# Rows for the experts gathered as quarter rows and turned in 32x32 blocks by VectorE

## The reference, cut to what matters

```python
def grouped_expert_mlp(h, expert, weight, w_gu, w_down):
    ...
    def expert_block(args):
        idx, e = args
        gate, up = jnp.split(h_pad[idx] @ w_gu[e], 2, axis=-1)
        return (jax.nn.silu(gate) * up) @ w_down[e]

    y = lax.map(expert_block, (slot_tok.reshape(n_blocks, MOE_BLOCK), block_e))
    y = y.reshape(-1, d) * slot_w[:, None]
    return jnp.zeros((n + 1, d), y.dtype).at[slot_tok].add(y)[:n]
```

## Time and profile before

| what | value |
|---|---|
| median of three runs | 2658.21 us |
| lowest, highest | 2656.98, 2659.9 us |
| profiled execution, span from first to last instruction | 2660.6 us |
| TensorE busy | 2561.7 us (96%) |
| VectorE busy | 1203.4 us (45%) |
| ScalarE busy | 562.7 us (21%) |
| GpSimd busy | 324.8 us (12%) |
| DMA | 590.71 MB, mean 222 GB/s |

### The profile page before, as it was taken

How to read it: one execution, slowest core, us unless ns; L and a number is a source line. 1 busy time by engine, 2 the same in 40 slices (tenths; PEclk the granted TensorE clock), 3 DMA queues, 4 the chain that set the end, 5 groups by cost and what they waited for, 6 DMA issues and landing times.

```text
span 2660.6 us, 34138 instructions
## 1 busy us (share of the span) xinstructions
PE 2561.7 (96%) x13314; PEld 1294.0 (49%) x13314; DVE 1203.4 (45%) x2576; ACT 562.7 (21%) x1181; POOL 324.8 (12%) x395
## 2 busy tenths in 40 slices
PE   6999999999999899999999899999999999999997
PEld 3444456547655444433333344577745444444333
DVE  3264357238777632222222475677787611111114
ACT  3211111028632100000000221488721000000002
POOL 0043200212011100000000012000011000000002
PEclk9999999999999999999999999899999999999998
DMA  9710111123123799999998810300024799999997
GB/s 381 306 17 0 67 48 61 35 37 88 59 104 126 292 398 420 414 378 373 411 394 334 347 51 0 71 2 2 1 76 160 271 390 423 417 423 417 407 417 263
DMA packets 99885, 590.71 MB, mean 222 GB/s; under 512 B 21727, under 2 KB 25015, under 8 KB 74761
## 3 DMA queue, kind: packets, MB, share of 16 engines
q1 hardware_dynamic: 81832, 535.72, 51.4%
q0 software_dynamic: 15296, 43.31, 4.1%
q10 hardware_dynamic: 2592, 9.44, 0.9%
HBM read 554.98 MB, written 45.99 MB: 226 GB/s over the span
## 4 chain that ended last, share of the span: by engine, by line
PE 84%; DMA 7%; DVE 6%; SPq 1%; issue 1%; POOL 0%; ACT 0%; POOLq 0%; DVEq 0%; ACTq 0%
PE PS L2702 34%; PE PS L1054 11%; PE PS L1250 5%; PE PS L1906 5%; PE PS L2139 4%; PE PS L1918 4%; PE PS L1929 4%; PE PS L1440 4%; PE PS L1723 4%; DMA ar<-in_expert_w_gu_dram 3%; DMA ar<-in_ada_w_dram 1%; PE PS L2707 1%; DMA ar<-yd 1%; DMA h2d<-ar 1%; PE PS L2712 1%
## 5 line engine op out<-in xcount | busy, mean ns | idle before, releaser
L2702 PE MATMUL PS<-ar 128*32 128x512 f32 (+2 forms) x4608 | 1012.5, 595 | 20.3 <-DMA ar<-in_expert_w_gu_dram 14.8
L2702 PEld LDWEIGHTS PS<-ar 128*32 128x32 f32 (+2 forms) x4608 | 372.2, 137 | 624.2 <-issue 616.9
L1054 PE MATMUL PS<-ar 128*128 128x512 f32 (+1 forms) x768 | 314.0, 565 | 4.2 <-DMA ar<-in_swa_w_in_dram 2.3
L2847 ACT ACTIVATE ar<-PS 128x512 f32<-128x512 f32 x48 | 28.7, 597 | 1068.3 <-PE PS L2702 1068.3
L1054 PEld LDWEIGHTS PS<-ar 128*128 128x128 f32 x768 | 144.2, 191 | 150.3 <-issue 141.5
L1962 DVE CUSTOM_DVE_ANT_0 ar<-PS,ar 128x640 f32<-128x640 f32 (+2 forms) x208 | 158.0, 797 | 71.5 <-PE PS L1906 71.3
L2139 PE MATMUL PS<-ar 128*128 128x512 f32 x392 | 175.2, 597 | 1.5 <-ACT ar L2270 0.9
L2919 DVE TENSOR_TENSOR ar<-PS,ar 128x512 f32<-128x512 f32 x48 | 33.2, 692 | 315.2 <-ACT ar L2847 315.2
L2942 DVE TENSOR_TENSOR ar<-PS,ar 128x1024 f32<-128x1024 f32 x48 | 58.8, 1225 | 242.2 <-PE PS L2702 137.1
L2925 DVE COPY ar<-PS 128x512 f32<-128x512 f32 x48 | 33.2, 692 | 279.7 <-PE PS L2712 279.7
L2017 ACT ACTIVATE ar<-ar 128x641 f32<-128x641 f32 (+4 forms) x208 | 159.5, 772 | 0.8 <-DVE ar L1962 0.8
(11 more groups left out here) (342 smaller groups left out, 2506.1 us busy)
## 6 DMA issues: line engine op xcount, KB each, us to landing
ar<-in_expert_w_gu_dram SPq DMA_DIRECT2D x128, 2048.0 KB, 16.1
ar<-in_expert_w_down_dram SPq DMA_DIRECT2D x64, 2048.0 KB, 15.5
ar<-in_ada_w_dram SPq DMA_DIRECT2D x24, 2048.0 KB, 14.7
ar<-yd SPq DMA_DIRECT2D x36, 512.0 KB, 5.4
ar<-in_ab_w_in_dram SPq DMA_DIRECT2D x6, 2048.0 KB, 9.3
h2d<-ar ACTq DMA_DIRECT2D x18, 512.0 KB, 2.9
ar<-in_x_dram SPq DMA_DIRECT2D x8, 512.0 KB, 13.5
ar<-in_ab_w_out_dram SPq DMA_DIRECT2D x1, 4096.0 KB, 27.0
```

What stands on the lines that cost most here:

```text
L1054: mm = nc.tensor.matmul(out_, lhs, rhs, start=(k == 0), stop=(k == KC - 1))
L2702: mm = nc.tensor.matmul(out[at:to], lhsT[:, at:to], w[:, k, cols], start=start, stop=stop)
```

## The change

From block 2 on a block's rows come in quarters. `h2d` is seen as 5120 rows of 1 KB. Four indirect DMAs fill `hb`: number j brings, to partition 32a + m, quarter a of the row of slot 32j + m. One VectorE transpose of 32x32 blocks then makes `hbT` of it, in place of eight transposes of TensorE and a copy from PSUM. The quarter row numbers are 4 x row + a; they are made once per layer: VectorE spreads `src_i` by a table, TensorE adds it up over the partitions (`route_fold`, four small products), and VectorE writes `src4_i` (`route_quarters`). The gated values are turned in SBUF by sixteen VectorE transposes of 32 partitions by 128 columns, in place of four of TensorE and a copy; only the last block of each layer keeps the old way. Blocks 0 and 1 keep the old way for their rows. `h2q`, `srcq` and `src4_i` are new; three small tables are added to the constants, and the semaphore counts follow.

```diff
             def turn(b):
-                pe.wait_ge(*done(f"{n}_hb{b % 2}", 16 * (b // 2 + 1)))
+                pe.wait_ge(*done(f"{n}_hb{b % 2}", hb_in(b)))
...
                 gate(b)
                 if b == 0:
                     route_shift(pe, l)
-                if b >= 1:
-                    turn_gu(b - 1)
-                if b + 1 < nb:
-                    turn(b + 1)
+                if b == 0:
+                    turn(1)
                 up(b)
+                if b == 0:
+                    route_fold(pe, l)
                 if b >= 1:
                     down(b - 1)
             if l == 1:
-                gate(nb - 1, lambda: turn_gu(nb - 2))
+                gate(nb - 1)
...
             def rows_in(b):
+                if b >= 2:
+                    dve.wait_ge(*done(f"{n}_hb{b % 2}", hb_in(b)))
+                    dve.wait_ge(*done(f"{n}_gu", b - 1))
+                    V.transpose(hbT[b % 2].rearrange("p k (j m) -> p k j m", j=4), hb[b % 2].rearrange("p (j m k) -> p k j m", j=4, k=KC))\
+                        .then_inc(S(f"{n}_hbT"), 1)
+                    return
...
             def gu_in(b):
-                dve.wait_ge(*done(f"{n}_gt", b + 1))
+                if b == nb - 1:
+                    dve.wait_ge(*done(f"{n}_gt", 1))
+                    dve.wait_ge(*done(f"{n}_dn", b - 1))
+                    V.tensor_copy(guT[b % 2].rearrange("p k n -> p (k n)"), PS[:, 4, :]).then_inc(S(f"{n}_guT"), 1)
+                    return
+                dve.wait_ge(*done(f"{n}_mul", b + 1))
                 if b >= 2:
                     dve.wait_ge(*done(f"{n}_dn", b - 1))
-                V.tensor_copy(guT[b % 2].rearrange("p k n -> p (k n)"), PS[:, 4, :]).then_inc(S(f"{n}_guT"), 1)
+                for j in range(4):
+                    m = slice(32 * j, 32 * j + 32)
+                    for a in range(4):
+                        last = V.transpose(guT[b % 2][32 * a:32 * a + 32, :, m], gub[b % 2][m, P * a:P * a + P].rearrange("p (m k) -> p k m", k=4))
+                last.then_inc(S(f"{n}_guT"), 1)
...
             mul(0)
+            gu_in(0)
+            route_quarters(dve, l)
...
             for b in range(1, nb - l):
-                gu_in(b - 1)
                 if b + 1 < nb:
                     rows_in(b + 1)
                 mul(b)
+                if b < nb - 1:
+                    gu_in(b)
                 result(b - 1)
...
+            def gather_quarters(b):
+                pool.wait_ge(*done(f"{n}_hbT", b - 1))
+                c = moe.blocks[b]["col"]
+                for j in range(4):
+                    pool.indirect_dma_start(out=hb[b % 2][:, 256 * j:256 * j + 256], out_offset=None, in_=h2q,
+                                            in_offset=bass.IndirectOffsetOnAxis(ap=src4_i[:, 4 * c + j:4 * c + j + 1], axis=0),
+                                            bounds_check=4 * TOK - 1, oob_is_err=False)\
+                        .then_inc(S(f"{n}_hb{b % 2}"), 16)
```

and in `route_slots`, `route_fold` and `route_quarters`:

```diff
-            slot_places(dve, ch, Vb, src_i[:, 0:nb], dst_i[:, 0:nb], key[:, 0:nb], nb, 0).then_inc(S(f"{n}_idx"), 1)
+            ch(slot_places(dve, ch, Vb, src_i[:, 0:nb], dst_i[:, 0:nb], key[:, 0:nb], nb, 0))
+            V.tensor_tensor(srcq[:, 0:4 * nb].rearrange("p (b j) -> p b j", j=4), bcast_in(src_i[:, 0:nb], 4),
+                            bcast_mid(cst[:, C_QUAD:C_QUAD + 4], nb), ALU.mult).then_inc(S(f"{n}_idx"), 1)
...
+            for a in range(4):
+                mm = nc.tensor.matmul(PS[32 * a:32 * a + 32, 7, 128:128 + 4 * n_blk[l]], cst[:, C_FOLD:C_FOLD + 32], srcq[:, 0:4 * n_blk[l]],
+                                      start=True, stop=True)
...
+            nc.vector.tensor_scalar(src4_i[:, 0:4 * n_blk[l]], PS[:, 7, 128:128 + 4 * n_blk[l]], 4.0, cst[:, C_PART:C_PART + 1], ALU.mult, ALU.add)\
+                .then_inc(S(f"r{l}_idx"), 1)
```

More of the change, by code:

```diff
@@ L61 @@
 C_KEY = C_SL + P
-C_N = C_KEY + 32
+C_FOLD = C_KEY + 32
+C_QUAD = C_FOLD + 32
+C_PART = C_QUAD + 4
+C_N = C_PART + 1
 def rank_bounds(l):
@@ L333, in program @@
         share(("{}_h2o",), "o0", "o1", 16 * NT)
-        share(("{}_cnt", "{}_first", "{}_ord", "{}_perm", "{}_shift", "{}_idx", "{}_ctl"), "r0", "r1", 1)
+        share(("{}_cnt", "{}_first", "{}_ord", "{}_perm", "{}_ctl"), "r0", "r1", 1)
         share(("{}_wx",), "r0", "r1", 2)
@@ L387, in program, with hb_in @@
         n_blk = [len(moe_blocks(l)) for l in range(2)]
+        def hb_in(b):
+            return 16 + 64 * (b // 2)
         kept = {Moe(1).pieces[i]["buf"] for part in "gud" for i, _, _ in Moe(1).at[part, n_blk[1] - 1]}
         yg[1] += [[R(piece_at[q] + 2048 * h + 1024 * j, D) for j in range(2)] for q in range(6) if q not in kept for h in range(2)]
-        share(("{}_tr", "{}_hbT", "{}_ga", "{}_gu", "{}_silu", "{}_mul", "{}_gt", "{}_guT", "{}_dn", "{}_y"), "m0", "m1", n_blk[0])
+        share(("{}_tr",), "m0", "m1", 2)
+        share(("{}_gt",), "m0", "m1", 1)
+        share(("{}_shift", "{}_idx"), "r0", "r1", 2)
+        share(("{}_hbT", "{}_ga", "{}_gu", "{}_silu", "{}_mul", "{}_guT", "{}_dn", "{}_y"), "m0", "m1", n_blk[0])
         for q in range(6):
@@ L393, in program @@
         for q in range(2):
-            share((f"{{}}_hb{q}", f"{{}}_yo{q}"), "m0", "m1", 16 * len(range(q, n_blk[0], 2)))
+            share((f"{{}}_yo{q}",), "m0", "m1", 16 * len(range(q, n_blk[0], 2)))
+            share((f"{{}}_hb{q}",), "m0", "m1", hb_in(n_blk[0] - 1 - (n_blk[0] - 1 - q) % 2))
         share(("{}_x",), "c0", "c1", NT)
@@ L419, in program @@
         for q, after in enumerate(("fx_in", "fx_out")):
-            share(("{}",), f"m1_hb{q}", after, 16 * len(range(q, n_blk[1], 2)))
+            share(("{}",), f"m1_hb{q}", after, hb_in(n_blk[1] - 1 - (n_blk[1] - 1 - q) % 2))
         for before, after in (("ss1", "fin_ss"), ("n1_ms1", "fin_ms"), ("n1_rt1", "fin_rt")):
@@ L2713, in gated_turned, with half_product @@
             return tr
-        def half_product(s, half, ws, amid=None):
+        def half_product(s, half, ws):
             for k in range(4):
-                if amid is not None and k == 2:
-                    amid()
                 for up in range(2):
@@ L2758, in turn, with gate @@
                 rows_turned(b % 2).then_inc(S(f"{n}_tr"), 1)
-            def gate(b, amid=None):
+            def gate(b):
                 pe.wait_ge(*done(f"{n}_hbT", b + 1))
@@ L2765, in gate @@
                     pe.wait_ge(*done(f"{n}_mul", b))
-                half_product(b % 2, 0, moe.weights(pe, "g", b), amid).then_inc(S(f"{n}_ga"), 1)
+                half_product(b % 2, 0, moe.weights(pe, "g", b)).then_inc(S(f"{n}_ga"), 1)
             def up(b):
@@ L2998, in gather @@
             def gather(b):
[L2999 to L3000 removed]
                 c = moe.blocks[b]["col"]
[L3002 to L3003 removed]
+                pool.indirect_dma_start(out=hb[b], out_offset=None, in_=h2d,
+                                        in_offset=bass.IndirectOffsetOnAxis(ap=first_i[:, c:c + 1], axis=0),
                                         bounds_check=TOK - 1, oob_is_err=False)\
[L3005 removed]
+                    .then_inc(S(f"{n}_hb{b}"), 16)
+            def gather_quarters(b):
[6 more added lines that the diff above has]
+                        .then_inc(S(f"{n}_hb{b % 2}"), 16)
             def scatter(b):
@@ L3016, in moe_pool @@
             gather(1)
-            pool.wait_ge(*done(f"r{l}_idx", 1))
+            pool.wait_ge(*done(f"r{l}_idx", 2))
             for b in range(2, nb):
-                gather(b)
+                gather_quarters(b)
                 if b >= 4:
```

21 lines of the change are left out of this document (11 added, 10 removed).

## The result

The changed kernel takes 2637.03 us (median of 4 runs, 2634.51 to 2644.53) against 2658.82 us (4 runs): ratio 0.9926, 95% interval 0.991 to 0.9943. It is 0.7% faster. Two later sets of 5 runs gave 0.9925 [0.9911, 0.9939] and 0.992 [0.9907, 0.9934]. The prediction said 2662, 3.8 us up, with 2641 as the lower end: the time moved the other way and lies outside the range. Where the time went, stage by stage, in profiled executions (us; the two repeats of after are in brackets).

A forecast was written before the change was run, and what follows sets the result against it. TensorE and DMA were taken as level, 22.3 us a block in layer 1. Layer 0 -7.7, layer 1 +8.1, clock +3.4: +3.8 on the profiled 2660.6, 2664.4, less 2.4 gives 2662; range 2641 to 2693.

The forecast's parts named there:

- The queue of the rows: Expert blocks: gathers and scatter need 45 software-queue turns, 27.4 us against 22.3, so rows come late; 4 and 6 us lost.
- The rival built on grouping: Both expert stages: quarter rows grouped to 4 KB a turn, rows never late; 2649 down to 2643, chance 0.27.
- the rows' lateness: Expert stages: DMA time lost while weights have no free buffer, 4 us in layer 0 and 6 in layer 1.
- the packets' cost: DMA engines: 432 more packets a block, 0.19 us a block, 4.5 us in layer 0 and 4.1 in layer 1.
- Layer 0's room: Layer 0 experts: 16.2 us of usable unused DMA time, less 4.5 for packets, gives 11.7 though TensorE frees 37.0.
- Layer 1: Layer 1 experts: no DMA time left from 2162 on; net +2.1 us before late rows, +8.1 with them.
- Clock: TensorE after stops: lower clock costs 1.7 us a stop; two that count, +3.4 us (0 to 12).
- VectorE: Each block: sixteen transposes 3.2 us, turn of rows 1.2 us, both hidden beside 20.7 us of products; cost 0.
- Start of a layer: First quarter gather waits for block 0's work; stop of 0 to 12 us once a layer, within the 4 and 6.
- The sum's base: Sum starts from the profiled 2660.6 us; the median of the runs taken as 2.4 below that span.

The follow-up runs named there:

- 48 turns: Changed kernel with three more indirect transfers that move no row ahead of each block's four gathers; 2659.03 us, ratio 1.0014 against the kernel before.
- the half loads: Changed kernel, each load into an expert weight buffer after the buffer's first bringing half its 2 MB; 2756.74 us (kernel before with the same loads: 2836.7).
- the doubled transposes: Changed kernel with each block's 16 VectorE transposes of the gated values made twice; 2654.23 us, ratio 0.9993 against the kernel before.

## Why the prediction was wrong

**The step that failed** is in "The queue of the rows": "After the change a block needs four gathers and a scatter, 45 turns", with "the four gathers are 36 turns". The four gathers are 12, the block's sum is 21, 12.8 us at 0.61 us a turn, against a period of 20.8. The rule that a turn is one packet, read from the earlier trace rows, held up (48 turns gave the landing that 45 were to give); that a packet is one row held only for rows of 4 KB, and the earlier trace rows could not show more, since every row there was whole. The Trainium skill (DMA: Bandwidth & Descriptors, Queues, rings and completion order) had it: a turn drains a whole packet of several descriptors. I took the single rows in the trace as its refutation, though a whole row of 4096 bytes fills such a packet (the Trainium skill, same title, section SWDGE vs HWDGE vs iDMA, gives a packet as preferably at most 4096 B and at most 64 descriptors); the software queue's packets of 4096 bytes above agree with it. The rival built on grouping, 2649 down to 2643, had the right mechanism and a chance of 0.27.

**The same error stood in the sum twice.** It gave the rows' lateness (4 + 6 us) and the packets' cost (4.5 + 4.1). Measured: 48 small packets more a block at 9 to 11 ns are 0.03 us on 16 engines, not 0.19. Both out, the sum is 3.8 - 18.6 = -14.8, or 2643.4; 6.4 above the measured 2637.0. With the forecast's own count of turns put in, the time was 2659.0, near the 2662, but that is luck. The landings came out as forecast (32.7 us where 33 was worked out) and TensorE stood for rows, yet in the dense stretches, where the sum had its 4 + 6 us, the stops cost nothing: 457.4 and 448.0 us against 456.4 to 460.3 and 447.1 to 448.9. The step from "rows late" to "DMA time lost" was not borne out either.

**Layer 0's room.** I took the idle share, 16.2 us in all and 0.04 x 335 = 13.4 for the long stretch. 14 to 22 came in all, 17 in the long stretch of the two profiles shown. Measured by rate, the 129 MB of that stretch at the 424 GB/s of the earlier trace rows are 304 us, a room of 31, of which little more than half was used. So the share was the nearer figure, a little low, and the rate is a ceiling. In the first profile of after TensorE stood for weights seven times in layer 0, the last time at 1290 us; behind it the blocks took 20.6 to 20.9 us each, and TensorE set the pace. Why the stretch stayed at 406 GB/s isn't shown.

**Layer 1.** Right that nothing was to be had: 505.1 and 505.9 us, share 1.00 before and after. TensorE's 33.9 us turned into stops (28.2 us for weights in place of 12.3, and 4.2 for rows) and slower products.

**Clock.** The term of +3.4 has no place in layer 1. TensorE's clock did fall (0.98 in the long stretch of layer 1 where it was 1.00), and beside the half loads layer 1 has 46.5 us more, of which stops for weights and rows are 32.7; the other 14 are slower products. Yet the layer took what it took before, at DMA share 1.00 in both: slower products added nothing to it. What the clock cost in layer 0 isn't shown.

**VectorE.** Priced too low (3.2 for 6.6, 1.2 for 2.0) and hidden, as said, behind the first blocks of a layer. The prediction had no word on what VectorE's time costs at the start of a layer by itself; there it is bare, as the doubled transposes show (+5 and +7 us).

**Start of a layer.** "A stop of 0 to 12 us once a layer": 2.5 us in the first profile and none in the two others in layer 0, none in layer 1.

**The sum's base.** The prediction took the profiled span as 2.4 us above the runs' median. Runs take some 1.8 us more than their spans, so that execution was about 4 us longer than the median, and part of the layer times read from it is chance.

**Not foreseen at all:** 3 to 6 us at the end of the kernel, a seventh to a quarter of the gain, still unexplained.

## What to carry to other kernels

Where two resources are level, ask of each stretch which of them has room, and take the room of the DMA engines as at least about their idle share and at most what bytes over the best rate seen in the kernel leave (13 and 31 us here, 17 used). Before pricing smaller transfers by a count of rows, find out how rows are grouped into packets: a trace in which every row fills a packet says nothing on it. A stop that a profile shows needn't cost its length: ask what else the engine would have stood for. An engine with half its time free can still be bare at the start of a stage, where its first results release the first transfers.

## What the runs showed of the hardware

- Indirect transfers of 1 KB rows go out four to a packet of 4096 bytes and cost the DMA engines what whole rows cost: 161 ns a packet against 160. Indices out of bounds are entries of 4 bytes, in packets of their own for 4 KB rows (9 ns), four to a packet for 1 KB rows (11 ns).
- 5279 packets of 4 bytes more in 300 us are 48 us of engine time out of 4800, yet beside packets of 16 KB on the weights' queue they made a gather land after 32.7 us and a scatter after 35.8, in place of 10.8.
- A VectorE transpose within blocks of 32 took 402 ns for 32x128 and 2034 ns for 128x1024 with the strides used here, in fp32. The second is 1.7 times the 1225 ns of the copy from PSUM that it replaces.
